# The 1/rms of a decoder step's final norm: from logarithm, exponential and refinement to a power on GpSimd

## What is computed

```python
def rmsnorm(x, g):
    xf = x.astype(jnp.float32)
    y = xf * lax.rsqrt(jnp.mean(xf * xf, axis=-1, keepdims=True) + EPS)
    return (y * g.astype(jnp.float32)).astype(x.dtype)

def layer_tail(x, ...):
    ...
    x = x + merged @ w_o
    h = rmsnorm(x, g_ffn)
    return x + (jax.nn.silu(h @ w_gate) * (h @ w_up)) @ w_down
...
    y_prompt = rmsnorm(yp, g_final)
    y_sample = rmsnorm(ys, g_final)
```

## Time and profile before

| | us |
|---|---|
| median of 3 runs | 1822.82 |
| lowest, highest | 1822.68, 1823.83 |
| the profiled execution | 1823.2 |
| its span, first to last instruction | 1820.8 |

### The profile page before, as it was taken

The page is one execution under the profiler, slowest core; times in us unless marked ns, Lnnn a source line. Parts: engine busy times, 40 slices in busy tenths (PEclk is TensorE's granted clock), DMA queues, the critical chain, the costliest instruction groups (busy, mean ns, idle before and its releaser), DMA issues.

```text
span 1820.8 us, 30848 instructions
## 1 busy us (share of the span) xinstructions
PE 1805.1 (99%) x12757; PEld 1777.5 (98%) x12757; DVE 955.6 (52%) x1337; ACT 679.5 (37%) x944; POOL 45.0 (2%) x131
## 2 busy tenths in 40 slices
PE   9999999999999999999999999999999999999997
PEld 8999999999999999999999999999999999999996
DVE  8755464465446445655544444444444444444455
ACT  6333333334333353444433333333333333333353
POOL 3010010000001000000000000000000000000000
PEclk9999999999999999999999999999999999999998
DMA  7484474557447444544444455444554435544443
GB/s 256 156 255 162 141 243 151 173 180 221 160 139 239 155 150 159 199 148 154 141 156 146 129 152 172 149 151 126 153 174 150 151 122 153 167 159 143 136 144 113
DMA packets 130829, 297.05 MB, mean 163 GB/s; under 512 B 16290, under 2 KB 59826, under 8 KB 130690
## 3 DMA queue, kind: packets, MB, share of 16 engines
q1 hardware_dynamic: 122096, 283.76, 49.0%
q10 hardware_dynamic: 7570, 8.78, 1.3%
q0 software_dynamic: 1024, 2.54, 0.5%
HBM read 284.88 MB, written 10.14 MB: 162 GB/s over the span
## 4 chain that ended last, share of the span: by engine, by line
PE 99%; DVE 0%; DMA 0%; ACT 0%; DVEq 0%; SPq 0%; issue 0%
PE banks L1194 31%; PE banks L1196 31%; PE banks L1195 31%; PE banks L1207 3%; PE banks L1204 1%; DMA weights_raw<-in_w_project 0%; PE banks L1424 0%; PE banks L1425 0%; PE banks L1426 0%; PE banks L1300 0%; DVE gates L1181 0%; DVEq L136 0%; PE banks L1224 0%; DVE weights_low L1066 0%; ACT weights_high L670 0%
## 5 line engine op out<-in xcount | busy, mean ns | idle before, releaser
L757 DVE TENSOR_TENSOR weights_low<-weights_raw,weights_high 128x1024 fp32r<-128x1024 f32 (+2 forms) x524 | 599.2, 1144 | 542.1 <-ACT weights_high L524 538.9
L524 ACT ACTIVATE weights_high<-weights_raw 128x1024 fp32r<-128x1024 f32 (+2 forms) x524 | 518.8, 991 | 648.8 <-PE banks L1196 647.0
L1194 PE MATMUL banks<-a_high,weights_high 128*128 128x320 f32 x2208 | 696.0, 315 | 0.0
L1196 PE MATMUL banks<-a_high,weights_low 128*128 128x320 f32 x2208 | 682.3, 309 | 0.0
L1195 PE MATMUL banks<-a_low,weights_high 128*128 128x320 f32 x2208 | 682.1, 309 | 0.0
L1194 PE MATMUL banks<-b_high,weights_high 128*128 128x320 f32 x1664 | 514.4, 309 | 0.0
L1196 PE MATMUL banks<-b_high,weights_low 128*128 128x320 f32 x1664 | 514.2, 309 | 0.0
L1195 PE MATMUL banks<-b_low,weights_high 128*128 128x320 f32 x1664 | 514.2, 309 | 0.0
L1194 PEld LDWEIGHTS banks<-a_high,weights_high 128*128 128x128 f32 x2208 | 414.7, 188 | 10.1 <-issue 8.9
L1195 PEld LDWEIGHTS banks<-a_low,weights_high 128*128 128x128 f32 x2208 | 415.0, 188 | 0.3
L1196 PEld LDWEIGHTS banks<-a_high,weights_low 128*128 128x128 f32 x2208 | 414.5, 188 | 0.0
(11 more groups left out here) (237 smaller groups left out, 657.0 us busy)
## 6 DMA issues: line engine op xcount, KB each, us to landing
weights_raw<-in_w_gate_up SPq DMA_DIRECT2D x176, 512.0 KB, 3.3
weights_raw<-in_w_project SPq DMA_DIRECT2D x156, 512.0 KB, 3.5
weights_raw<-in_w_down_a SPq DMA_DIRECT2D x64, 384.0 KB, 3.1
weights_raw<-in_w_down_b SPq DMA_DIRECT2D x64, 320.0 KB, 2.9
weights_raw<-in_w_merge SPq DMA_DIRECT2D x32, 512.0 KB, 3.3
weights_raw<-in_w_out SPq DMA_DIRECT2D x32, 512.0 KB, 3.3
area<-in_cache_kT SPq DMA_DIRECT2D x128, 64.0 KB, 3.0
area<-in_cache_v SPq DMA_DIRECT2D x128, 64.0 KB, 2.3
```

What stands on the lines that cost most here:

```text
L524: act.activation(high[:, u % SLOTS, 0:n], raw[:, u % SLOTS, 0:n], ACT.Copy).then_inc(on["high_ready"], 1)
L757: dve.tensor_tensor(low[:, u % SLOTS, 0:n], raw[:, u % SLOTS, 0:n], high[:, u % SLOTS, 0:n].bitcast(F32), ALU.subtract).then_inc(on["low_r ...
L1194: pe.matmul(bank(b, 0, T), w_high, x_high[:, k, :], start=first and n == 0, stop=False, skip_group_check=True)
L1196: done = pe.matmul(bank(b, 0, T), w_low, x_high[:, k, :], start=False, stop=last and n == tiles - 1, skip_group_check=True)
```

## The change

The two signals `y_sum_read` and `y_rstd_rough` become `y_mean_ready` and `y_rstd_ready`. ScalarE no longer takes part in the 1/rms and no longer loads the table set in the last chunk. VectorE waits for TensorE's sum, writes mean + eps to `mean` and signals GpSimd, which raises it to the power of -0.5, held in a tile of 320 columns, `minus_half`; VectorE then waits for that and multiplies.

```diff
@@ parts of area
         hidden = part(2560, T)
+        minus_half = part(2880, T)
@@ GpSimd, after the eight heads
+            pool.wait_ge(on["fox_out_read"], FH)
+            link(pool.memset(minus_half, -0.5))
+            pool.wait_ge(on["y_mean_ready"], 1)
+            pool.tensor_tensor(rstd, mean, minus_half, ALU.pow).then_inc(on["y_rstd_ready"], 1)
             pool.wait_ge(on["lf_stored"], 16)
@@ ScalarE, last chunk and end
-                    if final and s == 4 * CT + 1:
-                        act.preload_act_table_set("natural_log_exp_and_others")
                     if final and s >= 4 * CT + 2 and s % 2 == 0:
                         y_feature((s - 4 * CT) // 2 - 1)
             y_feature(KT - 1)
-            act.wait_ge(on["y_spread"], 1)
-            act.wait_ge(on["eps_ready"], 1)
-            act.activation(rstd, bank(2, 0, T), ACT.Ln, scale=1.0 / D, bias=eps[:, :]).then_inc(on["y_sum_read"], 1)
-            act.wait_ge(on["y_sum_read"], 1)
-            act.activation(rstd, rstd, ACT.Exp, scale=-0.5).then_inc(on["y_rstd_rough"], 1)
@@ VectorE, end
             down_read(CHUNKS - 1, KT - 1, True)
-            dve.wait_ge(on["y_sum_read"], 1)
-            link(dve.tensor_scalar(mean, bank(2, 0, T), 1.0 / D, EPS, ALU.mult, ALU.add))
-            dve.wait_ge(on["y_rstd_rough"], 1)
-            link(dve.tensor_tensor(rtmp, mean, rstd, ALU.mult))
-            link(dve.scalar_tensor_tensor(out=rtmp, in0=rtmp, scalar=-0.5, in1=rstd, op0=ALU.mult, op1=ALU.mult))
-            link(dve.scalar_tensor_tensor(out=rstd, in0=rtmp, scalar=1.5, in1=rstd, op0=ALU.add, op1=ALU.mult))
+            dve.wait_ge(on["y_spread"], 1)
+            dve.tensor_scalar(mean, bank(2, 0, T), 1.0 / D, EPS, ALU.mult, ALU.add).then_inc(on["y_mean_ready"], 1)
             dve.wait_ge(on["y_feat_ready"], KT)
+            dve.wait_ge(on["y_rstd_ready"], 1)
             for g, (m, n) in enumerate(Y_PIECES):
```

More of the change, by code:

```diff
@@ L120 @@
 sum_ready sum_spread ffn_mean_ready ffn_rstd_rough gate_ready silu_ready hidden_ready hidden_high_ready hidden_low_ready
-resid_final y_square_ready y_feat_ready y_sum_ready y_spread eps_ready y_sum_read y_rstd_rough
+resid_final y_square_ready y_feat_ready y_sum_ready y_spread eps_ready y_mean_ready y_rstd_ready
 y_ready_0 y_ready_1 y_ready_2 y_ready_3
```

## The result

| | before | changed |
|---|---|---|
| median | 1822.75 us (6 runs) | 1871.78 us (6 runs) |
| span of the profiled execution | 1820.8 us | 1870.0 us |
| GpSimd busy | 45.0 us | 96.7 us |

The ratio is 1.0269, 95% interval 1.0258 to 1.0279: slower by 49.0 us. The direction and the place were forecast, the size was not: 6.4 us were forecast and 21.2 was the most that the range allowed.

What follows compares the result with a forecast made beforehand. TensorE was taken to bound the kernel to 1806 us, then a chain of single steps. Mean 0.49 + 0.10 + power 8.3 + 0.19 = 9.08 us replaced 2.72: +6.4, so 1829.2 us, range 1821.5 to 1844.0.

Steps and rivals of the forecast that it cites:

- What bounds the kernel, and the replaced stretch: TensorE works almost without a gap to 1806.0 us; behind it, logarithm to refinement take 2.72 us, a ceiling on the gain.
- the tail: From the first large multiplication of y to the end: 9.7 us, left as it is and moving as a whole.
- The table load: ScalarE's 1.28 us load at 1731.23 us goes; the time saved becomes idle time, price 0, no other load takes its place.
- The mean moves forward, the fill: VectorE's mean starts at the sum's end, 1808.38 us, taking 0.49; GpSimd's fill of `minus_half` ends early, price 0.
- The hand-overs: Last chain: VectorE to GpSimd taken as 0.10 us, GpSimd back to VectorE as 0.19 us.
- The plain operation on GpSimd: Lower bound for the power: an addition of two tensors, 2.3 ns a column, 0.90 us for 320 columns.
- The power itself: GpSimd's 128x320 power in the last chain: 8.3 us taken, between 0.90 and 23.1 us.
- X - 1.94: Change in kernel time when the power takes X us in the last chain; +6.4 us at 8.3 us.
- the nine passes: Estimate of GpSimd's power: logarithm and exponential as three passes each, nine at 0.90 us, 8.1 us in all.
- One column after another, each step waiting for the last: Rival for GpSimd's power: 13 us and more, 23.1 us at 72 ns a column, time 1844.0 us; 13 to 23 us: 0.17.
- no ceiling of the trace above 23: Case of GpSimd's power taking above 23 us, with no ceiling that the trace gives; chance 0.12, left out of the range.
- signs of a wrong mechanism: TensorE's last products starting later than 1807.5 us, a ScalarE table load in the last stage, or a tail no longer 9.7 us.

## Why the prediction was wrong, step by step

- **What bounds the kernel, and the replaced stretch.** Right. TensorE's work to 1806 us is unchanged, 2.72 us of chain went, and the tail, 9.70 us before, is 9.62 to 9.67 in the changed kernel and all the experiments. This is what shows that it moves as a whole; the 3.1 to 3.5 us of the earlier trace rows are those of ScalarE's two stores alone, not of all four.
- **The table load.** Right that it is worth nothing. ScalarE's timeline after, to be set beside the earlier trace rows:

```profile
1729.85 0.47 ACT L732 ACTIVATE a_high<-area 128x320 fp32r<-128x320 f32 x1 [3.83 <-DVEq L1159]
...
1731.33 0.85 ACT L529 ACTIVATE weights_high<-weights_raw 128x768 fp32r<-128x768 f32 x1 [0.38 <-PE banks L1191]
1734.15 0.47 ACT L662 ACTIVATE area<-gates 128x320 f32<-128x320 f32 x1 [1.98 <-DVEq L1053]
```

  The load is gone and no other has come in. Of its time 0.78 us is now in the waits (0.38 and 1.98 us, where 1.58 stood), and the square behind them comes half a microsecond earlier than the rest of the shift would bring it. TensorE has nothing of that: the changed kernel's execution was 0.26 us ahead already before the load (1729.85 against 1730.11), and it is 0.27 us ahead at the last sum (1807.27 against 1807.54). That start moves by some tenths from kernel to kernel anyway: it is 1807.92 and 1807.04 in two experiments that both have the table load (logarithm and exponential on three columns, with a shared bank and with three).
- **The mean moves forward, the fill.** Right: at the sum's end to 0.04 us; the fill took 0.37 us at 631 us.
- **The hand-overs.** 0.10 and 0.19 assumed, 0.15 and 0.11 measured. The sum without the power is 0.75 us instead of 0.78.
- **The plain operation on GpSimd.** 0.90 us from the slope of two sizes in the earlier trace rows; 0.88 and 0.86 measured for a multiplication of that shape.
- **The power itself.** This step failed: "I take 8.3 us", with an upper bound of 72 ns a column and 23.1 us. It takes 159.8 ns a column and 51.5 us. With X = 51.5 the formula of the prediction, X - 1.94, gives +49.6, and +49.0 was measured; so the mechanism and the rest of the sum hold and this one term was too small by a factor of six. Three things were wrong in it. The upper bound was a row of another function, a selection of 8 columns; a row of another function bounds nothing from above. Nor was it the dearest row per column, as the prediction says: the trace before has fills of a single column on GpSimd that take 105 ns, which at that rate gives 34 us for 320 columns. Nearly all of that is fixed cost, since a fill of 320 columns takes 0.36 us; a rate from a short instruction says little of a long one, upwards or downwards. And the nine passes counted a logarithm or an exponential as three additions; measured against the addition's slope of 2.3 ns a column in the earlier trace rows, a whole power is some seventy additions.
- **The rivals.** "One column after another, each step waiting for the last" had 13 us and more at 0.17, and no ceiling of the trace above 23 at 0.12. It is in the latter that the result fell. The runs show the strict proportion to columns; that steps within a column wait for each other is not shown. The estimate worked out there with the figure of the Trainium skill, GPSIMD Engine Reference, section on pitfalls (4 cycles for each dependent step) and fifteen steps of my own came to 16 us; by the same page's figures, 4 cycles at 1.2 GHz, a chain would need about 48 such steps to reach 160 ns a column, which is an estimate. No run here counts the steps.
- **What would show it.** The gap from the mean's end to the first multiplication was forecast as 8.6 us and is 51.8: a size error by the test that the prediction gave itself, and none of its signs of a wrong mechanism is there.

The range should have been open above. The trace showed no power on any engine, and the sum turned on it alone; 0.12 for "no ceiling" was too little beside a bound that was borrowed.

## What to carry to other kernels

A function that an engine has never run in the trace has no upper bound there: measure it alone, on an engine that idles beside the bound, before it is put on the last chain; here GpSimd worked 455 us more in such a run and the time stayed. For a power on GpSimd count the columns, not the rows: numbers that are repeated over rows should be held once, 128 to a column, which turned 51.5 us into 0.9. The way back over all rows has its own price, 0.88 or 1.54 us here by TensorE's clock. And before changing a chain, work out what a free step would bring: 1.11 us of 1822 was the most here, so the bet had little to win.

## What the runs showed of the hardware

- A power of two fp32 tensors on GpSimd: 0.36 us and 159.8 ns a column, for 1, 16 or 128 rows, within 0.4 us at 320 columns for exponents -0.5, 0.5, 1 and 2, and on the first call of an execution as on later ones. A multiplication of 128x320 takes 0.88 us.
- Such a power, 51.5 us long, disturbs neither TensorE nor the time of the kernel when it runs beside the feed-forward: VectorE was busy for 154.40 us in 316 where it was 153.78.
- A product that starts in one column of a PSUM bank, issued while sums in other columns of that bank were open, took their first part away: with a bank for each column the sums were whole, with a shared one only the column started last was. The Trainium skill, PSUM — Partial Sum Buffer, section on the four PSUM rules, has this: a starting product clears the marks of the whole bank, so that the next product on the other columns overwrites instead of adding. These runs agree.
- Three small products on TensorE (six pieces) after 1.3 us of idle time took 0.88 us in two runs and 1.54 in two others, at granted clocks of 1.00 and 0.50, with the same work before. The clock had fallen during that wait, at its start in one run and behind its middle in the other.
